# First layer's output projection: four of its eight tiles as split products of high and low parts

## The reference, cut to what matters

```python
y = jnp.concatenate([rms_norm(merge_heads(o_dil), og_dil),
                     rms_norm(merge_heads(o_moba), og_moba),
                     rms_norm(merge_heads(o_mem), og_mem)], axis=-1) @ w_out
x = x + y
x = x + peer_ffn(rms_norm(x, g_ffn), w_peer_q, sub1, sub2, peer_u, peer_v)
```

## Time and profile before

| | us |
|---|---|
| median of 3 runs | 1931.25 (1930.73 to 1932.47) |
| the profiled execution, its own time | 1932.39 |
| its span, first to last instruction | 1930.7 |
| PE busy | 1899.4 (98%) |
| DVE busy | 1501.1 (78%) |
| ACT busy | 1157.9 (60%) |
| mean granted TensorE clock | 0.999 |

### The profile page before, as it was taken

One profiled execution on the slowest core, in us unless ns is written; L12 is line 12 of the kernel. 1 busy time (PEld: TensorE's weight loads), 2 busy tenths in 40 slices (PEclk: granted clock), 3 DMA queues, 4 the chain that ended last, 5 costly groups with the idle time before them and its releaser, 6 DMA issues.

```text
span 1930.7 us, 38686 instructions
## 1 busy us (share of the span) xinstructions
PE 1899.4 (98%) x12752; PEld 1728.6 (90%) x12752; DVE 1501.1 (78%) x3609; ACT 1157.9 (60%) x2442; POOL 233.6 (12%) x262
## 2 busy tenths in 40 slices
PE   9899999999999999999999999999999999999998
PEld 8779999999888899999989898998889989998886
DVE  6676798888778878888888487877887568887776
ACT  5645666998444444544466577655557567765555
POOL 1000695665000000000000000010000000010000
PEclk9999999999999999999999999999999999999999
DMA  8446555444775588777757533565665553455552
GB/s 309 153 171 236 179 174 169 139 150 137 255 254 192 198 312 288 280 281 291 263 206 262 197 131 121 171 212 191 248 246 177 186 175 121 139 179 175 185 191 103
DMA packets 109463, 388.33 MB, mean 201 GB/s; under 512 B 12160, under 2 KB 16528, under 8 KB 108304
## 3 DMA queue, kind: packets, MB, share of 16 engines
q1 hardware_dynamic: 95040, 335.40, 50.6%
q10 hardware_dynamic: 8096, 28.70, 4.3%
q0 software_dynamic: 6192, 22.55, 3.2%
HBM read 379.76 MB, written 6.82 MB: 200 GB/s over the span
## 4 chain that ended last, share of the span: by engine, by line
PE 86%; DVE 9%; ACT 2%; DVEq 2%; issue 1%; DMA 0%; ACTq 0%; SPq 0%
PE bank L763 13%; PE bank L771 12%; PE bank L768 12%; PE bank L1002 7%; PE bank L1008 7%; PE bank L1005 7%; PE bank L1405 5%; PE bank L1069 3%; PE bank L1402 2%; PE bank L901 1%; PE bank L1214 1%; DVE part_lo L2159 1%; PE bank L1263 1%; ACT part_hi L1473 1%; DVE arena L2388 1%
## 5 line engine op out<-in xcount | busy, mean ns | idle before, releaser
L1473 ACT ACTIVATE part_hi<-ring 128x512 fp32r<-128x512 f32 x1124 | 692.0, 626 | 369.8 <-PE bank L768 162.6
L2159 DVE TENSOR_TENSOR part_lo<-ring,part_hi 128x512 fp32r<-128x512 f32 (+1 forms) x764 | 507.6, 685 | 158.0 <-ACT part_hi L1473 148.8
L763 PE MATMUL bank<-u_hi,part_hi 128*128 128x256 f32 (+1 forms) x1888 | 545.2, 289 | 4.9 <-POOL part_lo L2061 3.4
L771 PE MATMUL bank<-u_hi,part_lo 128*128 128x256 f32 (+1 forms) x1888 | 529.8, 281 | 0.0
L768 PE MATMUL bank<-u_lo,part_hi 128*128 128x256 f32 x1808 | 505.8, 280 | 0.0
L763 PEld LDWEIGHTS bank<-u_hi,part_hi 128*128 128x128 f32 (+1 forms) x1888 | 354.7, 188 | 13.2 <-POOL part_lo L2061 4.6
L771 PEld LDWEIGHTS bank<-u_hi,part_lo 128*128 128x128 f32 (+1 forms) x1888 | 356.8, 189 | 0.0
L768 PEld LDWEIGHTS bank<-u_lo,part_hi 128*128 128x128 f32 x1808 | 339.7, 188 | 3.1
L1002 PE MATMUL bank<-part_hi,w_hi 128*128 128x512 f32 x688 | 269.1, 391 | 0.2 <-DVE w_lo L2488 0.2
L1008 PE MATMUL bank<-part_lo,w_hi 128*128 128x512 f32 x688 | 268.0, 389 | 0.0
L1005 PE MATMUL bank<-part_hi,w_lo 128*128 128x512 f32 x688 | 267.9, 389 | 0.0
(11 more groups left out here) (354 smaller groups left out, 3223.5 us busy)
## 6 DMA issues: line engine op xcount, KB each, us to landing
ring<-stream_dram SPq DMA_DIRECT2D x606, 512.0 KB, 3.3
arena<-ada_dram ACTq DMA_DIRECT2D x54, 512.0 KB, 4.7
arena<-ada_dram POOLq DMA_DIRECT2D x42, 512.0 KB, 4.5
acts_kept<-act SPq DMA_DIRECT2D x32, 128.0 KB, 3.6
arena<-acts_kept SPq DMA_DIRECT2D x4, 1024.0 KB, 5.4
xT<-x_dram SPq DMA_DIRECT2D x4, 256.0 KB, 5.4
arena<-mem_dram SPq DMA_DIRECT2D x1, 1024.0 KB, 9.1
arena<-keys_dram SPq DMA_DIRECT2D x1, 1024.0 KB, 8.2
```

The costliest lines, as they stand in the source:

```text
L763: m = pe.matmul(o, hi, u(cc), start=first, stop=False)
L771: m = pe.matmul(o, lo, u(cc), start=False, stop=last)
L1473: act.activation(part_hi[:, h % 4, 0:width], ring[:, n % RING, (h % 2) * width:(h % 2 + 1) * width], ACT.Copy).then_inc(hi_ready, 1)
L2159: v.tensor_tensor(part_lo[:, h % 4, 0:width], ring[:, n % RING, (h % 2) * width:(h % 2 + 1) * width], part_hi[:, h % 4, 0:width], ALU.subt ...
```

## The change

Tiles 4 to 7 of the output projection become split products. ACT makes a high part of each chunk of `oT` (in `u_lo`) and DVE the low part (in `x_lo`); ACT and DVE split the eight half-slabs. Where these operations are put on ACT and DVE is part of the diff. The counters of halves behind them move by eight (`MIX_HALVES`).

```diff
+MIX_PLAIN = 4
...
-PQ_HALVES = V_HALVES + 2 * (PEER_Q - PQ_PLAIN)
+MIX_HALVES = V_HALVES + 2 * (W_OUT1 - MIX_PLAIN)
+PQ_HALVES = MIX_HALVES + 2 * (PEER_Q - PQ_PLAIN)
...
-            for j in range(4, 8):
-                mix_part(j, range(DC), True, True)
+            for j in range(MIX_PLAIN, M_OUT1):
+                for h in (2 * (j - MIX_PLAIN), 2 * (j - MIX_PLAIN) + 1):
+                    m = passes(h, V_HALVES, lambda c: (bank[j][:, 0:S], c == 0, c == DC - 1),
+                               lambda c: u_lo[:, c, :], lambda c: x_lo[:, c, :],
+                               (og_chunk, DC) if j == MIX_PLAIN else None)
+                m.then_inc(mix_full, 1)
                 if j == 5:
                     pe.wait_ge(mix_taken, 4)
...
             inverse_root_of(wgt2[:, 1, :], wgt2[:, 0, :], bank[4][:, 0:S], 1.0 / 256).then_inc(og_root, 1)
+
+            def mix_high(h):
+                split_half(S_OUT1 + MIX_PLAIN + h // 2, h, 0, V_HALVES)
+
             for c in range(DC):
+                if c in (3, 5):
+                    mix_high(c // 2 - 1)
+                act.wait_ge(og_chunk, c + 1)
+                act.activation(u_lo[:, c, :], oT[:, c, :], ACT.Copy).then_inc(og_root, 1)
+            mix_high(2)
+            mix_high(3)
+            for c in range(DC):
+                if c >= MIX_PLAIN:
+                    for h in {4: (4,), 5: (5, 6), 6: (7,), 7: ()}[c]:
+                        mix_high(h)
                 act.wait_ge(mix_taken, c + 1)
                 square(sq[:, c, :], xT[:, c, :]).then_inc(p_sq, 1)
...
             take_group(2)
             for n in range(6, 8):
                 modulation_early(n)
+            def mix_low(h):
+                rest_of_half(S_OUT1 + MIX_PLAIN + h // 2, h, V_HALVES)
+
+            for c in range(DC):
+                if c in (3, 5):
+                    mix_low(c // 2 - 1)
+                v.wait_ge(og_root, 3 + c + 1)
+                v.tensor_tensor(x_lo[:, c, :], oT[:, c, :], u_lo[:, c, :], ALU.subtract).then_inc(og_chunk, 1)
+            mix_low(2)
+            mix_low(3)
             v.wait_ge(pos_loaded, 16)
...
                 v.tensor_tensor(xT[:, j, :], bank[j][:, 0:S], xT[:, j, :], ALU.add).then_inc(mix_taken, 1)
                 if j in (3, 4):
                     turn_table(j - 3)
+                for h in {3: (4,), 4: (5,), 5: (6, 7)}.get(j, ()):
+                    mix_low(h)
                 if j == 4:
                     v.drain().then_inc(turn_ready, 1)
                 if j in (5, 6):
                     modulation_early(2 * j - 2)
                     modulation_early(2 * j - 1)
```

More of the change, by code:

```diff
@@ L968, in _ @@
                 for h in (2 * (j - PQ_PLAIN), 2 * (j - PQ_PLAIN) + 1):
-                    m = passes(h, V_HALVES, lambda c: (b[:, 0:S], c == 0, c == DC - 1),
+                    m = passes(h, MIX_HALVES, lambda c: (b[:, 0:S], c == 0, c == DC - 1),
                                lambda c: u_hi[:, c, :], lambda c: u_lo[:, c, :],
@@ L1600, in query_high @@
             def query_high(h):
-                split_half(S_PQ + PQ_PLAIN + h // 2, h, 0, V_HALVES)
+                split_half(S_PQ + PQ_PLAIN + h // 2, h, 0, MIX_HALVES)
             query_high(0)
@@ L2350, in _ @@
                     modulation_early(2 * j - 1)
-            rest_of_half(S_PQ + PQ_PLAIN, 0, V_HALVES)
+            rest_of_half(S_PQ + PQ_PLAIN, 0, MIX_HALVES)
             v.wait_ge(row_ready, 1)
@@ L2362, in _ @@
             scale_query(0)
-            rest_of_half(S_PQ + PQ_PLAIN, 1, V_HALVES)
+            rest_of_half(S_PQ + PQ_PLAIN, 1, MIX_HALVES)
             for c in range(DC):
@@ L2367, in _ @@
             scale_query(1)
-            for h in range(2, PQ_HALVES - V_HALVES):
-                rest_of_half(S_PQ + PQ_PLAIN + h // 2, h, V_HALVES)
+            for h in range(2, PQ_HALVES - MIX_HALVES):
+                rest_of_half(S_PQ + PQ_PLAIN + h // 2, h, MIX_HALVES)
                 if h % 4 == 3 and h < 16:
```

## The result

| | before | after |
|---|---|---|
| median, 7 runs each | 1931.85 us | 1939.92 us |
| lowest to highest | 1930.73 to 1932.47 | 1936.45 to 1940.69 |
| ratio after to before | | 1.0039, 95% interval 1.0028 to 1.0049 |
| profiled execution, its span | 1930.7 us | 1936.7 us |
| mean granted TensorE clock, profiled | 0.999 | 0.996 |

The change makes the kernel 8 us slower, 0.4%. The forecast was 6.3 us more. The profiled execution took 1938.39 us, 1.53 less than the median. The PE is busy for 1901.3 us of its span and was for 1899.4, so most of the loss is in waits.

The account below looks back on a forecast made before the run. The PE was taken to bound the kernel, with DVE coming last after the change. DVE's queue delays the row of squares by 6.3 us, PE saving included; added to the 1931.25 us median this gives 1937.6 us, range 1933.0 to 1941.5.

Parts of the forecast that it names:

- second rival: Output projection: the PE clock falls in its idle gaps, adding 3 us to the forecast, 1940.7 us; chance 0.14.
- The sum, 6.3 us: Output projection: the row of squares ends at 163.55 in place of 157.25, and the shift carries to the kernel's end.
- PE on half 2 from 143.75: Tile 5: the PE starts half 2 after slab 45 lands and is split, 1.46 us later than before.
- half 4 at 150.5: Tile 6: the PE starts at 150.5, after turn table 0 and low half 4 on DVE.
- half 5 at 154.7: Tile 6: the PE starts half 5 after turn table 1 and low half 5 on DVE, ending at 156.1.
- row of squares 163.55: End of the output projection: the PE's last sum ends at 163.55 in place of 157.25.
- turn table 1's end at 153.85: DVE in the projection: turn table 1 runs from 150.6 for 3.24 us, then low half 5 takes 0.69.
- Low parts before slab 45 hidden: DVE before tile 4: 3.95 us of low parts cost nothing, hidden behind the PE's tiles 0 to 3.
- 1.34 us of idle: PE waiting for slab 45 before the change: the clock stayed at 1.00, counted against the second rival.
- The gaps on the PE: Output projection: the change makes four idle stretches on the PE, of 3.4, 3.0, 2.8 and 1.2 us.
- Slab 45 at 7.59 us: Tile 5's load: lands 7.59 us after its unmoved request, at 142.24; called the least certain term.
- The PE's saving, 0.73 us a tile: Tiles 4 to 7: split 2.83 us against plain 3.56; 2.9 us for four, at most 2.2 left after waits.

Follow-up runs that it names:

- x8_order_only: x7_best2 with slab 45 asked for late again, as in the kernel before, and low half 2 ahead of the adds; 1931.79 us, ratio 0.9996.
- x9_early_warm: x5_early_slab_split with idle products filling its two PE gaps, 8 before half 4 and 11 before half 5; 1933.76 us, ratio 1.0006.
- x2_adds_first: Changed kernel with DVE's positions and adds of tiles 0 to 3 put ahead of slab 45's low halves; 1936.63 us, ratio 1.0022.
- x0_after: The changed kernel run again unaltered, as yardstick against the kernel before; 1940.10 us, ratio 1.0039.
- x1_warm: Changed kernel with idle products filling the PE's three gaps, 14, 12 and 11 before halves 2, 4 and 5; 1938.03 us, ratio 1.0030.
- x3_late_work: Changed kernel with both turn tables and modulations 8 to 11 moved behind the projection, between query halves; 1938.35 us, ratio 1.0032.
- x4_early_slab_plain: Kernel before, all tiles plain, with slab 45 asked for earlier, at tile 0's first group; 1931.25 us, ratio 0.9995.
- x7_best2: x6_best with modulation 7 moved behind the last add and modulation 8 into the query halves; 1928.79 us, ratio 0.9979.
- x5_early_slab_split: Changed kernel with slab 45 asked for earlier, at tile 0's first group, DVE's order untouched; 1935.10 us, ratio 1.0016.
- x6_best: Changed kernel with slab 45 asked for early and adds, turn tables and modulations reordered on DVE; 1928.62 us, ratio 0.9982.

## Why the prediction was right

The direction, the place and the mechanism came out as written, and the range held the time. The forecast's own figure, 1937.6 us, came out less well: the median of 1939.92 is nearer to the 1940.7 of the second rival.

- *The sum, 6.3 us.* The profile shows 6.18 (6.59 less the 0.41 of the stages ahead). Step by step: PE on half 2 from 143.75, measured 144.02; table 0 from 146.3, measured 146.61; half 4 at 150.5, measured 150.70; half 5 at 154.7, measured 154.88; last add 162.05, measured 162.31; row of squares 163.55, measured 163.84. Take off the 0.41 and each is right within 0.3. This is the execution in which the low clock cost nothing. One step was right without its working: from turn table 1's end at 153.85 the terms named (low half 5, add 5, low halves 6 and 7: 0.34 and three times 0.60) give 156.0, and the prediction writes 157.15. In the trace the way is 3.26 us (154.14 to 157.40), and 0.80 of it is DVE's wait for ACT's high half 7, where the prediction held ACT to be ahead.
- *Low parts before slab 45 hidden:* right, the PE's first split product stands at 137.55 and tile 4 has no gap.
- *The order, not the number of instructions:* shown by x8_order_only, which does all the split work with the request where it was, and is no slower than before. Order and landing go together: against before, the old order costs 8.0 us with the late request and 2.8 with the early one, the new order -0.75 and -3.75. Of the 6.2 us in the first profile, 1.7 are left when the slab is early and the clock held (x9_early_warm), and some 2.1 are the adds behind slab 45 (x2_adds_first). The other 2.4 are had only by subtraction: DVE waits for the slab with the turn tables behind it.
- *The clock.* The step that was off is the chance of the second rival: I held the clock's fall to be one case in seven, to add 3 us. It is in every profile of a kernel with an unfilled gap of 2 us or more, and its cost runs from none (first profile) to 2.5 us (x0_after). The median carries 2.1 of it by x1_warm, about the difference between the 6.3 forecast and the 8.0 measured. So forecast and second rival were both true, not one or the other, and x0_after lost its time where the rival had put it, from half 5 on. The rival's price of a product was too high: their starts lie 0.213 us apart at 0.50, not 0.236. The Trainium skill, "TensorE: Matmul & The Clock Gate", Part 1, has the idle PE fall back to 1.2 GHz and regain 2.4 with activity; the trace agrees, with 0.50 from 144.0 after the gap of 3.28 us and 1.00 again by 148, though in x0_after the fall came 1.3 us after the PE had begun again. That 1.34 us of idle had not touched it was weak evidence against.
- *The gaps on the PE:* forecast 3.4, 3.0, 2.8 and 1.2 us; measured 3.28, 1.29, 1.32 and 0.84. The second and third were shorter, since the half clock stretched the tiles in front of them.
- *Slab 45 at 7.59 us, as its request doesn't move:* right in the changed kernel (7.53 and 7.83 in its two profiles, 7.37 in x1_warm, 7.28 in x2_adds_first). As a rule it was too firm: with the same requests it was 4.14 in x3_late_work. What decides it is open. Of the modulation slabs that POOL asks for, one goes out 1.1 us before it and one 0.15 after (133.92 and 135.21 beside 135.06); in x8_order_only neither does, the one before at 129.90, and slab 45 took 3.17. But x3_late_work has both beside it (133.58 and 134.87 beside 134.72) and took 4.14, so they don't decide it alone.
- *The PE's saving, 0.73 us a tile:* oversized. Between two sums, a plain tile and its sums take 4.34 us (144.81 to 149.15 in x4_early_slab_plain), a split one 3.74 (143.64 to 147.38 in x7_best2): 0.60 a tile. For four that is 2.4 us, and 2.39 is the distance of the two copies (157.93 and 155.54). The split tile was undersized: it takes 2.95 us between the end of one pair of sums and the next (144.43 to 147.38), where 24 times the pitch of 0.118 gave 2.83; the pitch inside a half leaves out its ends.

## What to carry to other kernels

Cheaper products need parts made by other engines, and where an engine works in program order the place of each new instruction counts for more than its length: an instruction that waits for a load must not stand in front of work that is ready, and independent fill work belongs behind the last instruction that the bound engine waits for, as far as the stage behind has room for it (in x3_late_work it had not: over 3 us were lost there). Before replacing a form of product, list for each half when its parts are made, by name of the instruction in front. Where a chain hangs on one load, ask first whether the load can be asked for earlier: one edited line took 5.2 us off here. When a change opens gaps on the PE, count the clock too: it fell in all five profiles with a gap of 2.05 us or more, and also behind gaps of 1.29 and 1.61 us. Fill the gaps, or better, close them.

## What the runs showed that was not expected

- 37 idle products in gaps made the changed kernel 2.1 us faster (x1_warm against x0_after), though in the first profile the low clock was wholly hidden.
- The clock fell also after gaps far shorter than the first: in the first profile it is at 0.50 from 151 on, with a gap of 1.29 us in front of half 4, where the PE had done only sums of one column since 148.5. In x5_early_slab_split it fell at about 147.4 with no gap above 1.61 us before it. In x8_order_only, with one gap of 1.50 us, it did not fall.
- The same load, with the same requests in front of it, took from 4.1 to 7.8 us to land. Kernels that wait for it long spread over 4 us (x1_warm, x8_order_only), the kernel before, which waits 1.34 us, over 1.3 to 3.0, those that don't wait over 1.0 to 2.0 (x6_best, x7_best2, x9_early_warm, x4_early_slab_plain). That the landing is the cause is argued from these pairs; it was not varied by itself.
- In the profile of x5_early_slab_split one of the ring's loads in the query tiles took 13.03 us to land (189.22 to 202.25); the PE stood idle 0.57 us for the parts made from it.
